# A mixer and expert layer on one core: three fixed experts, heavy units spread over rounds of nine, rotary halves swapped by DMA

## What is computed

```python
q = _rope(q.reshape(b, s, 8, 64), cos, sin)    # x1*c - x2*s | x2*c + x1*s, halves of 32 channels
k = _rope(k.reshape(b, s, 2, 64), cos, sin)
...
x = x + gate1 * mixer(h)                       # attention, state space, Fourier, short convolution
scores = sigmoid(t @ w_router)                 # 32 experts in 8 groups: best group, two experts in it
y[token] += weight * ((silu(t @ w1[e]) * (t @ w3[e])) @ w2[e])
```

## Time and profile before

| | us |
|---|---|
| median of 3 runs (lowest, highest) | 1171.25 (1169.71, 1171.6) |
| profiled execution, its own time | 1170.8 |
| its span, first to last instruction | 1169.0 |
| TensorE busy | 1099.4 (94%) |
| VectorE busy | 561.8 (48%) |
| ScalarE busy | 316.8 (27%) |
| POOL busy | 167.3 (14%) |
| mean granted clock of TensorE | 0.991 |
| weight loads of the expert stage | 28 of each matrix, 2048 KB |
| chain that ended last | TensorE 77%, DMA 10%, VectorE 7% |

### The profile page before, as it was taken

How to read it: one execution, slowest core, us unless ns; L and a number is a source line. 1 busy time by engine, 2 the same in 40 slices (tenths; PEclk the granted TensorE clock), 3 DMA queues, 4 the chain that set the end, 5 groups by cost and what they waited for, 6 DMA issues and landing times.

```text
span 1169.0 us, 16277 instructions
## 1 busy us (share of the span) xinstructions
PE 1099.4 (94%) x5701; PEld 706.3 (60%) x5701; DVE 561.8 (48%) x1010; ACT 316.8 (27%) x539; POOL 167.3 (14%) x237
## 2 busy tenths in 40 slices
PE   6999999999999999999999998899999999888775
PEld 4788878878667777778888777333333333332223
DVE  5776677753676778766554446221211111111114
ACT  4642322234434554342433242100000000000003
POOL 0000000000110223355000100122222122122110
PEclk9999999999999999999999998999999999999998
DMA  9423646630111222223132559989999999999985
GB/s 384 188 105 120 227 148 230 228 115 13 60 51 59 72 73 73 91 72 129 70 109 90 190 234 353 427 350 408 427 425 425 425 425 425 427 426 425 426 365 227
DMA packets 41335, 278.16 MB, mean 238 GB/s; under 512 B 7482, under 2 KB 7994, under 8 KB 29376
## 3 DMA queue, kind: packets, MB, share of 16 engines
q1 hardware_dynamic: 34496, 264.95, 56.6%
q0 software_dynamic: 6784, 12.49, 2.9%
HBM read 274.11 MB, written 13.40 MB: 246 GB/s over the span
## 4 chain that ended last, share of the span: by engine, by line
PE 77%; DMA 10%; DVE 7%; ACT 3%; issue 2%; POOL 0%; SPq 0%; DVEq 0%; POOLq 0%; ACTq 0%
PE psum L702 73%; DMA ering<-in_wb 7%; DMA expert_rows<-ysb,idx 2%; PE psum L718 1%; DVE amx L1802 1%; DMA xr<-token_rows,tabt 1%; DVE sc L1791 1%; DVE ring_lo L1531 1%; PE psum L1044 1%; ACT ring_hi L1232 1%; PE psum L740 1%; DMA Hx<-in_xT 1%; ACT gth L1232 0%; DVE amx L1803 0%; DVE ytmp L1531 0%
## 5 line engine op out<-in xcount | busy, mean ns | idle before, releaser
L702 PE MATMUL psum<-ering,xs 128*64 128x512 f32 x1056 | 235.7, 597 | 10.2 <-DMA ering<-in_wb 7.8
L702 PE MATMUL psum<-Hhi,ring_hi 128*128 128x512 f32 x472 | 189.4, 401 | 0.1
L702 PE MATMUL psum<-Hlo,ring_hi 128*128 128x512 f32 x472 | 185.3, 393 | 0.2 <-DVE Hlo L1531 0.2
L702 PE MATMUL psum<-Hhi,ring_lo 128*128 128x512 f32 x472 | 183.2, 390 | 0.0
L702 PEld LDWEIGHTS psum<-ering,xs 128*64 128x64 f32 x1056 | 73.9, 137 | 155.3 <-issue 136.5
L1531 DVE TENSOR_TENSOR ring_lo<-ring,ring_hi 128x1024 fp32r<-128x1024 f32 x87 | 107.0, 1230 | 111.8 <-ACT ring_hi L1232 110.7
L702 PE MATMUL psum<-ering,at 128*64 128x512 f32 x528 | 119.4, 597 | 7.3 <-ACT at L1232 6.1
L1232 ACT ACTIVATE ring_hi<-ring 128x1024 fp32r<-128x1024 f32 x87 | 92.2, 1060 | 75.0 <-DMA ring<-in_stream 44.9
L1531 DVE TENSOR_TENSOR ysb<-psum,G 128x512 f32<-128x512 f32 x33 | 22.8, 691 | 171.8 <-DMA expert_rows<-ysb,idx 120.5
L1531 DVE TENSOR_TENSOR sg<-sg,psum 128x256 f32<-128x256 f32 x66 | 27.7, 420 | 160.6 <-ACT sg L1232 159.4
L702 PEld LDWEIGHTS psum<-Hhi,ring_hi 128*128 128x128 f32 x472 | 88.7, 188 | 23.3 <-issue 4.0
(11 more groups left out here) (353 smaller groups left out, 1454.5 us busy)
## 6 DMA issues: line engine op xcount, KB each, us to landing
ering<-in_w SPq DMA_DIRECT2D x28, 2048.0 KB, 14.3
ering<-in_wb SPq DMA_DIRECT2D x28, 2048.0 KB, 20.0
ering<-in_wa SPq DMA_DIRECT2D x28, 2048.0 KB, 16.3
ring<-in_stream SPq DMA_DIRECT2D x87, 512.0 KB, 4.2
ada_ring<-in_stream SPq DMA_DIRECT2D x32, 512.0 KB, 3.8
ada<-in_adaw SPq DMA_DIRECT2D x4, 2048.0 KB, 10.6
Am<-decay_rows POOLq DMA_DIRECT2D x8, 512.0 KB, 4.2
gat<-expert_rows SPq DMA_DIRECT2D x4, 1024.0 KB, 8.0
```

What stands on the lines that cost most here:

```text
L702: return nc.tensor.matmul(out, lhsT, rhs, start=start, stop=stop)
```

## The change

1. **Three fixed experts** (FIXED = 3: experts 16, 17, 18). The third has fixed weights only; its tokens still come by gather (EARLY stays 2). Buffers move so that slot 2 is free sooner: `hA`, `dg`, `folded`, `vrow`, `pa`, `step`, `sml`, `tabd`, `tabt` lie elsewhere, partly over constants no longer needed, and the ring of stream tiles is turned by three places (TURN_RING) so that (0,0) lies under none of the last tile's places. SP's order becomes: (0,2), (1,1), (1,2), (2,1) after `merge_done`; (0,0) after `wo` 6; (0,1), (1,0) after `wo` 7; (2,0) after `ssq2`; (2,2) after the picks. The two loads of `gfr` move from the `wo` stage to behind `g2`.
2. **Rounds of nine units** (TRIO). Heavy units at places 5 and 8 of each nine: here 5, 8, 14, 17, 23. Engine loops run over 8 rounds of nine, with tests nested by nine, three and one; SP's loop keeps rounds of three, now up to 24. NTAB grows from 102 to 162 columns, MAXU from 45 to 72. n becomes the larger of the unit count and 4.5 nh + 1.5.
3. **Rotary swap by transfers.** `rot` is POOL's: four DMAs of 32 partitions by 2 KB each, from `ropet[:, i % 2]` to `ropet[:, 3]`, sign in the sine table; they wait for ScalarE's copy and for `rope_ready` of the rotation before. A new step `rope` for VectorE stands one tile later.
4. POOL's two clearings of `xr` go; the first scatters, which write nothing, read constants instead.

```diff
-        tile(("fu", m), *([("rot", 0)] if m == 1 else []))
+        tile(*([("rope", 0)] if m == 2 else []), ("fu", m), *([("rot", 0)] if m == 1 else []))
...
-        tile(("q", m), *([("rot", m)] if m else [("decr",)]))
+        tile(*([("rope", m - 1)] if m > 1 else []), ("q", m), *([("rot", m)] if m else [("decr",)]))
...
-        tile(("cg", m), *([("rot", 4)] if m == 0 else []))
-        tile(("sx", m))
+        tile(*([("rope", 3)] if m == 0 else []), ("cg", m), *([("rot", 4)] if m == 0 else []))
+        tile(*([("rope", 4)] if m == 0 else []), ("sx", m))
...
         early(1, 2)
+        early(2, 1)
+        job_full(sp, ("wo", KD - 2))
+        early(0, 0)
         job_full(sp, ("wo", KD - 1))
-        early(0, 0)
         early(0, 1)
         early(1, 0)
+        job_full(sp, ("ssq2",))
+        early(2, 0)
...
-        job_full(sp, ("bexp",))
-        sp.wait_ge(route_done, 1)
         job_full(sp, ("g2",))
-        e = sp.value_load(brow[0:1, EARLY:EARLY + 1], min_val=0, max_val=NE - 1)
-        chosen(EARLY, 0, e)
-        chosen(EARLY, 1, e)
+        for q in range(2):
+            sp.dma_start(gfr[q][:, :], gfin[:, q * S:q * S + S]).then_inc(const_in, 16)
         sp.wait_ge(h2_out, 16 * NCH)
         job_full(sp, ("pick", 1))
-        chosen(EARLY, 2, e)
+        early(2, 2)
...
-            elif k0 == "rot":
-                b = claim(pe, s)
-                job_read(pe, ("k",) if s[1] == 0 else ("q", s[1] - 1))
-                mm(bk(b), CT[:, C_PERM:C_PERM + P], ropet[:, s[1] % 2, :], True, True).then_inc(full[b], 1)
...
-            elif k0 == "rot":
+            elif k0 == "rope":
                 i = s[1]
-                job_full(v, s)
                 v.wait_ge(cs_in, 16)
...
                 link(TT(ropet[:, 2, :], ropet[:, i % 2, :], cs[:, 0, :], ALU.mult))
-                TT(ropet[:, 3, :], bk(b), cs[:, 1, :], ALU.mult).then_inc(*t(empty[b], plan[s][1]))
-                job_read(v, s)
+                v.wait_ge(turned_in, 64 * (i + 1))
+                link(TT(ropet[:, 3, :], ropet[:, 3, :], cs[:, 1, :], ALU.mult))
...
+            if k0 == "rot":
+                i = s[1]
+                job_read(g_, ("k",) if i == 0 else ("q", i - 1))
+                if i:
+                    g_.wait_ge(rope_ready, i)
+                for q in range(4):
+                    there = (q + 1 - q % 2 * 2) * 32
+                    G_.dma_start(ropet[q * 32:q * 32 + 32, 3, :], ropet[there:there + 32, i % 2, :]).then_inc(turned_in, 16)
...
-    heavy_at = unit % SLOTS == SLOTS - 1
+    heavy_at = (unit % SLOTS == SLOTS - 1) & (unit % TRIO >= SLOTS)
```

TensorE's loop after the change (the other engines' are cut the same way; `heavy` marks the places 5 and 8 of nine, `k` is the number of the next heavy unit):

```diff
+        with pe.Fori(0, MAXU // TRIO) as i:
+            with pe.If(i * TRIO + 1 < n):
+                for a in range(SLOTS):
+                    with pe.If(i * TRIO + a * SLOTS + 1 < n):
+                        for q in range(a * SLOTS, a * SLOTS + SLOTS):
+                            u, j = i * TRIO + q + 1, (q + 1) % SLOTS
+                            here, then = i * 48 + 16 * ((q + 1) // SLOTS + 1), i * 48 + 16 * ((q + 2) // SLOTS + 1)
+                            heavy, k = q in (4, 7), i * 2 + (q > 5)
+                            with pe.If(u < n):
+                                act_turn(0, u + 1)
+                                if heavy:
+                                    with pe.If(k < nh):
+
+                                        up_and_gate(1, j, k + 1, here)
+                                        tokens_in(1, k + 2)
+                                with pe.If(k >= nh):
+                                    down(0, j, u + 1, here)
+                                with pe.If(u + 1 < n):
+
+                                    up_and_gate(0, (j + 1) % SLOTS, u + 2, then, True)
...
```

More of the change, by code:

```diff
@@ L41 @@
 RING, HI_RING = 5, 3
+TURN_RING = 3
 ROUNDS = MAXU // SLOTS
 HALF = BLK // 2
[L44 to L47, removed]
+NTAB = 2 * (MAXU + TRIO)
+UM = 4 * NTAB
+UM_N = UM + 6
+EARLY, FIXED = 2, 3
 E0 = NE // 2
@@ L229, in bank_plan @@
             b = 1 + s[1] // 2
-        elif k in ("ynorm", "macc", "zk", "rtk", "dt", "csq", "xa", "seg"):
+        elif k in ("ynorm", "macc", "zk", "rtk", "dt", "csq", "xa", "seg", "rot", "rope", "seg"):
             continue
@@ L390, in build @@
     PT = [at("PT0", 73728 + 7680, [P, 640]), at("PT1", o, [P, 640])]; gf_at.append(o); o += 2560
+    step = at("step", 193728 + C_LE * 4, [P, 2 * NE])
+    bex = at("bex", o, [P, 2 * NE]); o += 256
     assert o <= 229368 - BASE, o
@@ L543, in lo_place @@
     def lo_place(x):
-        return ring_lo[:, raw_index[x] % RING, :]
+        return ring_lo[:, (raw_index[x] + TURN_RING) % RING, :]
     def arrived(eng, x):
@@ L920, in _ @@
                     ins.then_inc(zk_done, 1)
-            elif k0 == "rot":
-                b = claim(pe, s)
-                job_read(pe, ("k",) if s[1] == 0 else ("q", s[1] - 1))
-                mm(bk(b), CT[:, C_PERM:C_PERM + P], ropet[:, s[1] % 2, :], True, True).then_inc(full[b], 1)
+            elif k0 in ("rot", "rope"):
+                pass
             elif k0 == "dec":
@@ new lines, in _ @@
+        with pe.Fori(0, MAXU // TRIO) as i:
[16 more added lines that the diff above has]
+                                    up_and_gate(0, (j + 1) % SLOTS, u + 2, then, True)
+                                    if not heavy:
+                                        tokens_in(0, u + 1)
+                                if heavy:
+                                    with pe.If(k < nh):
+                                        act_turn(1, k + 1)
+                                    with pe.If(u + 1 < n):
+                                        tokens_in(0, u + 1)
+                                with pe.If(k < nh):
+                                    if heavy:
+                                        down(1, j, k + 1, here)
+                                    down(0, j, u + 1, here)
@@ L1985, in _ @@
                 rk = bk(b)[:, NE:NE + NCH * NE].rearrange("p (c n) -> p c n", n=NE)
-                cols_ = slice(E0, E0 + EARLY)
+                cols_, fixed = slice(E0, E0 + EARLY), slice(E0, E0 + FIXED)
                 v.wait_ge(y_out[0], 16)
@@ L2182, in _ @@
         g_.wait_ge(merge_done, 32)
-        for h in range(2):
-            G_.memset(xr[h][:, :], 0.0).then_inc(*t(pool_c))
-        t.settle()
         token_half = h2d.rearrange("s (a n) -> (s a) n", a=2)
@@ L2226, in _ @@
         for h in range(2):
-            gather_at(h, tabt[:, 2 * EARLY + h:2 * EARLY + h + 1])
+            first = (2 * EARLY, 4 * SLOTS - 1)[h]
+            gather_at(h, tabt[:, first:first + 1])
         for h in range(2):
             g_.wait_ge(xt_full[h], 1)
-            gather(h, (slice(2 * SLOTS, 2 * SLOTS + 1), slice(4 * SLOTS - 1, 4 * SLOTS))[h], 2)
+            gather(h, (slice(2 * SLOTS, 2 * SLOTS + 1), slice(2 * TRIO - 1, 2 * TRIO))[h], 2)
         g_.wait_ge(route_done, 3)
@@ L2364 @@
         a["router_bias"], _np.arange(32, dtype=_np.float32), _np.arange(8, dtype=_np.float32),
-        _np.arange(NTAB, dtype=_np.float32), _np.tile(rank, 2).astype(_np.float32),
+        _np.tile(rank, 2).astype(_np.float32),
         early_rank.reshape(-1).astype(_np.float32)])
```

220 lines of the change are left out of this document (105 added, 115 removed).

## The result

The changed kernel takes 1163.91 us (median of 6 runs, 1161.54 to 1166.52) for 1171.11 of the kernel before (6 runs beside it, 1169.71 to 1172.23): ratio 0.9943, 95% interval 0.9931 to 0.9956. Forecast: 1163.5, range 1158 to 1169.5. The profiled execution took 1165.77 us, its span 1163.9. The total came out within 0.4 us, but most of its terms didn't: their errors nearly cancel, and that is luck.

The account below looks back on a forecast made before the run. Weight traffic was taken to end the expert stage, TensorE to bound the rotary stage. From 1170.8 us, terms -3.0, -4.3 (table delay included) and -0.5 gave 1163.0, with the median's 0.45 1163.5; range 1158 to 1169.5.

Parts of the forecast that it names:

- Rotary: Rotary stage: five swaps off TensorE's path save 4.3 us, less a stall of 1.3; net -3.0, between -4.3 and +6.6.
- the stall of 1.3: TensorE's wait for the split of the second `sx` tile, delayed by serial swap cycles of 7.65 us: 1.3 us.
- The rule for the stall: Rotary stage: TensorE's stall is four swap cycles less 29.3 us of cover, never below 0.
- Nine chunks ahead: Weight queue before the expert stage: earlier loads gain nothing, since slots come free no sooner; 0 us.
- rival (b): Early chunks count in full: all idle DMA time, 15.5 us, comes off the end; 1152.3 us, chance 0.06.
- Bigger tables: Start of expert stage: wider table matmuls and casts make unit 2 and the freeing of (4,2) 1.3 us later.
- Light first: Expert stage: new unit order ends the last down-projection at 1138.0 for 1142.3; -4.3 us, table delay included.
- the transfers' gain of 6.2: Expert stage's DMA path: with no empty queue from (4,2) on, (5,2) is in at 789.8 for 796.0; 6.2 us.
- rival (c): The expert stage gives nothing: tables, gather and the late heavy unit eat the 6.2; 1167.8 us, chance 0.15.
- Tail: After the last down-projection: six empty loop rounds go, but the final gather's second block still arrives at 1154.7; -0.5 us.
- (a): Rival: no lag of the swaps, and DMA ends the expert stage; 1160.2 us, chance 0.15.
- (e): Rival: the third fixed expert has no token, so a 29th unit is added, +15.5; 1179 us, chance 0.03.

Follow-up runs that it names:

- x7: The changed kernel with POOL waiting for each of a tile's four rotary transfers before issuing the next; 1183.35 us, ratio 1.0115 to the kernel before.
- x2: The changed kernel with chunks (2,1) and (2,0) asked for late as before, and (0,0) one step later; 1166.33 us, ratio 0.9957.
- x9: x6 with chunks (2,1), (2,0) and (0,0) asked for as late as before; 1162.54 us, against 1160.22 for x6 in the same set.
- x5: The changed kernel with six more spare matmuls on TensorE ahead of its wait for the last gather; 1162.4 us, ratio 0.9921.
- x10: The kernel before with only the rotary changed to transfers, and gfin's loads counted on the constants' semaphore; 1163.51 us, ratio 0.9946.
- c2: The changed kernel, unchanged, run and profiled once more; 1162.81 us, ratio 0.9941 to the kernel before.
- c3: The same kernel as x10, run again in another set; 1166.76 us, ratio 0.9967 to the kernel before.
- x6: The changed kernel with heavy units at 5, 8, 11, 14, 17 and six more spare matmuls before the last gather; 1160.22 us, ratio 0.9922.

## Why the prediction was right, and where it wasn't

**Rotary, -3.0: mechanism right, size off.** The matmuls were worth their 4.3 (4.6 measured). The cycle was the term mis-sized: 5.35 us for 7.65, so the stall of 1.3 doesn't exist. Of the two ends of the landing I took the POOL store of the earlier trace rows, 3.4 us; the SP store's 2.1 was the right one. The estimate by the Trainium skill's fit (DMA: Bandwidth & Descriptors, "Anatomy of one DMA — SWDGE (gpsimd) path"), 2.15 us for 64 KB, agrees with the 2.1 measured. The Trainium skill's rule that VectorE in a two-port mode shuts GpSimd out of descriptor writing (SBUF — State Buffer, "SBUF: two separate sides") left no sign: POOL's issues took 0.50 us each, with VectorE busy 8.6 of the 10 us from 150 to 160. Whether any of VectorE's instructions there ran in such a mode no row says. The rule for the stall came within 2 us of the loss that x7 shows at the first load.

**Nine chunks ahead, 0: wrong.** Holes do appear where slots come free too late, at 725 and 740, and rival (b) is out by x2 and x9. But the step let the holes give everything back, because by the time of (4,2) "the old kernel too had loaded everything it was allowed to". It had not. (4,2) is asked for at 765.69, and the transfers of the kernel before are still full there; their hole comes at 774:

```profile
750.00:770.00 20.00, 18.04 (x80) 6.70 (x82) 3.65 (x7) 1.15 (x3) 5.88 (x9) 0.91 1.01 415
```

So two chunks less in that queue shorten it. By x2 and x9, 8 to 9 us of transfers are moved ahead and 6 to 6.5 come back as holes; 2.5 and 2.4 us of the expert stage are left.

**Bigger tables, +1.3: too much.** The table matmuls took 2.47 us, not 3.2; the gather's issue follows the stage's start by 11.18 us for 10.63, so 0.55 later. With two chunks fewer ahead of the gathers, they come sooner by more than that: unit 2's up-projection ends 30.3 us into the stage and (4,2) is asked for at 34.7, where the kernel before has 33.3 and 37.5. This is the step's own bound of 0, "if the gather then finds less traffic". In x2, without that relief, (4,2) is asked for at 37.8.

```profile
731.82 2.47 PE L701 MATMUL psum<-oneb,onep 128*128 128x162 f32 x16
```

**Light first, -4.3: right in the sum, wrong in its parts.** The expert stage lost 3.3 to 4.0 us, the last wait for weights ends at 1061.86 (forecast 1062.9 less the rotary's 3.0, used 1.75 later: 1061.7), and the last down-projection ended 4.1 us nearer to the first load. The step is the transfers' gain of 6.2 less TensorE's lag behind the late heavy unit, 1.9 (1138.0 less 1136.1). The runs have for the lag 2.3 (410.0 to 407.7, early loads) and 2.5 (412.6 to 410.1, late loads), and for the transfers 5.6 (413.3 to 407.7). But that 5.6 is the work of two edits: with unit 2's loads late it is 3.2 (413.3 to 410.1). So the transfers' gain, counted at 6.2 for the order alone, is 3.2 for the order and 2.4 for the early loads, which the step before had at 0. By itself the order with the last heavy unit at 23 brings 0.8 (413.3 to 412.6), less than the 1.8 by which the old order's own profiles spread and near to the nothing of rival (c); with the last one at 17 it brings 3.2.

One reading of the step is off without harm. Here a load needs nearer 1 us than 2.2 from issue to first bytes: after the one asked for at 725.08 in the changed kernel the DMA share, 0.06 from 725 to 726, is 0.93 from 726 to 727. The 2.2 stands on both sides of the 6.2 and drops out.

**Tail, -0.5: the step that failed.** It was bounded by +1 and became +2.4. It counted the idle time of the empty rounds as removed. That pause of 6.14 us had stood ahead of TensorE's transposes, and the clock fell and had risen again by the time the gathered blocks came. In the kernel before, windows from 1142:

```profile
1142.30:1148.40 6.10, 0.04 (x2) 0.00 (x0) 0.69 (x1) 0.00 (x0) 1.16 (x2) 0.69 0.10 34
1148.40:1152.50 4.10, 4.02 (x18) 3.23 (x19) 1.49 (x3) 2.27 (x4) 0.00 (x0) 0.63 0.99 368
1152.50:1156.00 3.50, 3.50 (x15) 2.08 (x15) 2.46 (x4) 2.83 (x7) 0.00 (x0) 1.00 1.03 425
```

With the rounds gone the transposes come sooner, the pause moves behind them, straight before the closing matmuls, and those run at the low clock. The first closing matmul comes 10.3 us after the end of the last down-projection in the kernel before (1152.60) and 10.0 in the changed one, ScalarE's squares 13.1 and 15.5: the loss lies between them. The gather takes 4.89 us from its issue in the changed kernel and 4.93 in x5, so it isn't the gather. x5 shows both halves: with the clock kept up the tail is 26.5, which is the forecast's 26.7 - 0.5 within 0.3.

So the terms' errors nearly cancel: the rotary 1.6 us better than its term, the early chunks 2.5 better, the order 3.5 worse, the tail 2.9 worse, 2.3 worse in sum. The time is only 0.4 above the forecast; the rest lies in the second stage (0.7) and within what single terms spread by. Of the rivals, (a) had the rotary right, with no stall; (e) is out, since 28 loads of each matrix ran.

## What to carry to other kernels

An idle time of TensorE that is taken out of a chain may only move; look at what runs right after its new place, because that is what pays for the low clock, and fill the pause with matmuls into a bank that is about to be overwritten. Loads moved into idle transfer time pay for what they fill less what comes back as holes; count both over the whole stage, and before pricing them at nothing check that the old queue had really run dry. A small transfer that waits in the same stretch (the gather here) may come sooner and still not be what the time shows. Price POOL-issued transfers inside SBUF by their own size and overlap, four in a row here for 3.4 us rather than four landings, and when terms of a sum are near the noise, read each from its own stage over several profiles, not from one median.

## What was not expected of the hardware

The router's stage, first load to first expert matmul, has two lengths whatever the kernel: 54.6 to 54.9 us in five profiles, 55.7 to 56.4 in nine, and both in one kernel (56.12 and 54.59 in the changed one, 54.80 and 56.39 in x10). The first group of pick matmuls on TensorE in the changed kernel and in its repeat c2:

```profile
713.54 4.55 PE L701 MATMUL psum<-ohs,h2t 128*128 128x128 f32 x24 [1.08 <-issue]
```

```profile
712.32 2.92 PE L701 MATMUL psum<-ohs,h2t 128*128 128x128 f32 x24 [1.09 <-issue]
```

The same 24 matmuls take 1.63 us more in the one: TensorE's granted clock is 0.72 from 712 to 716 in the one and 1.00 in the other, that is, partly at its lower level. This comes behind a string of short waits, and which matmuls it meets changes from one execution to the next. It is as large as the terms disputed here, and it may be one reason why two sets of one kernel (x10 and c3) differ by 0.002: their profiles differ by 1.6 us in this stage. Two more differences stay open: why the first load of the kernels with transfers spreads over 2.4 us when `pads` spreads over 0.9 (163.18 to 164.06), and why by the medians x6 shows less than its two stages add up to.
